# A two-block kernel: which engine does the side work of the last projection

## What is computed

```python
def swiglu_ffn(h, w_ffn_in, w_ffn_out):
    gate, up = jnp.split(h @ w_ffn_in, 2, axis=-1)
    return (jax.nn.silu(gate) * up) @ w_ffn_out

# last two lines of second_block
    y = swiglu_ffn(h, w_ffn_in[l], w_ffn_out[l])
    x = x + ga2 * rmsnorm(y, post_ffn_g[l])
```

## Time and profile before

| | |
|---|---|
| time, three runs | 1335.21 us median (1334.09 to 1336.07) |
| profiled execution | 1334.96 us, of which the span in the trace 1333.2 us |
| TensorE busy | 1313.8 us (99% of the span) |
| VectorE busy | 982.8 us (74%), 1218 instructions |
| ScalarE busy | 554.2 us (42%) |
| GpSimd busy | 88.2 us (7%) |
| granted TensorE clock | 0.999 of full (2.4 GHz) |

### The profile page before, as it was taken

One profiled execution on the slowest core, in us unless ns is written; L12 is line 12 of the kernel. 1 busy time (PEld: TensorE's weight loads), 2 busy tenths in 40 slices (PEclk: granted clock), 3 DMA queues, 4 the chain that ended last, 5 costly groups with the idle time before them and its releaser, 6 DMA issues.

```text
span 1333.2 us, 15857 instructions
## 1 busy us (share of the span) xinstructions
PE 1313.8 (99%) x6443; PEld 1065.8 (80%) x6443; DVE 982.8 (74%) x1218; ACT 554.2 (42%) x770; POOL 88.2 (7%) x153
## 2 busy tenths in 40 slices
PE   7999999999999999999999999999999999999997
PEld 4799688888888888888888777778878888888885
DVE  4787877999778777677759799866795444346988
ACT  4553444344333343222332566774443222224543
POOL 0000000000001000100000011000002210000001
PEclk9999999999999999999999999999999999999999
DMA  9544055325455546654222211122204333325565
GB/s 387 199 133 137 2 172 199 129 87 187 158 174 179 182 162 207 222 201 164 92 99 95 95 64 48 49 95 95 95 32 158 117 120 103 104 103 195 189 221 190
DMA packets 34473, 188.03 MB, mean 141 GB/s; under 512 B 4304, under 2 KB 5088, under 8 KB 18016
## 3 DMA queue, kind: packets, MB, share of 16 engines
q1 hardware_dynamic: 20976, 140.32, 29.7%
q0 software_dynamic: 13424, 46.69, 10.8%
HBM read 182.79 MB, written 4.20 MB: 140 GB/s over the span
## 4 chain that ended last, share of the span: by engine, by line
PE 84%; DVE 8%; ACT 3%; DMA 3%; issue 2%; SPq 0%; DVEq 0%; ACTq 0%
PE bank L1695 25%; PE bank L1697 24%; PE bank L1696 24%; DVE WL L947 2%; PE bank L2039 2%; PE bank L2040 2%; PE bank L2045 2%; DMA raw<-weights 1%; DMA adaf<-ada 1%; PE bank L1900 1%; DVE ada_acc L989 1%; PE bank L2235 1%; ACT WH L448 1%; PE bank L2205 1%; DVE raw L960 1%
## 5 line engine op out<-in xcount | busy, mean ns | idle before, releaser
L1695 PE MATMUL bank<-hH,WH 128*128 128x512 f32 x992 | 390.1, 393 | 0.9 <-DVE WL L947 0.5
L1697 PE MATMUL bank<-hH,WL 128*128 128x512 f32 x992 | 386.4, 390 | 0.0
L1696 PE MATMUL bank<-hL,WH 128*128 128x512 f32 x992 | 386.3, 389 | 0.0
L947 DVE TENSOR_TENSOR WL<-raw,WH 128x2048 fp32r<-128x2048 f32 (+1 forms) x114 | 253.6, 2227 | 153.8 <-ACT WH L448 153.7
L448 ACT ACTIVATE WH<-raw 128x2048 fp32r<-128x2048 f32 (+1 forms) x117 | 218.0, 1866 | 237.1 <-DMA raw<-weights 179.5
L1695 PEld LDWEIGHTS bank<-hH,WH 128*128 128x128 f32 x992 | 186.3, 188 | 42.5 <-issue 3.3
L1697 PEld LDWEIGHTS bank<-hH,WL 128*128 128x128 f32 x992 | 186.2, 188 | 39.4
L1696 PEld LDWEIGHTS bank<-hL,WH 128*128 128x128 f32 x992 | 186.4, 188 | 37.7 <-issue 0.2
L989 DVE SCALAR_TENSOR_TENSOR ada_acc<-ada_half,csil,ada_acc 128x1024 f32<-128x1024 f32 x70 | 89.7, 1281 | 4.9 <-DMA ada_half<-ada_later 2.3
L1444 DVE SCALAR_TENSOR_TENSOR cacc<-uT,vec,cacc 128x511 f32<-128x511 f32 (+29 forms) x120 | 83.3, 756 | 0.0
L401 POOL DMA_DIRECT2D ada_half<-ada_later x80 | 42.6, 532 | 569.7 <-DVE ada_acc L989 334.9
(11 more groups left out here) (360 smaller groups left out, 2176.8 us busy)
## 6 DMA issues: line engine op xcount, KB each, us to landing
raw<-weights SPq DMA_DIRECT2D x119, 1024.0 KB, 5.0
ada_half<-ada_later POOLq DMA_DIRECT2D x80, 512.0 KB, 4.5
adaf<-ada SPq DMA_DIRECT2D x8, 1024.0 KB, 19.8
xT<-x_t SPq DMA_DIRECT2D x4, 512.0 KB, 6.0
x_rows<-xB POOLq DMA_DIRECT2D x32, 64.0 KB, 2.2
gF<-x_rows POOLq DMA_DIRECT2D x3, 512.0 KB, 6.9
ctxT<-ctx_t SPq DMA_DIRECT2D x1, 1024.0 KB, 28.0
out_t<-gF SPq DMA_DIRECT2D x2, 512.0 KB, 2.6
```

Of the source, the lines that this page charges most:

```text
L947: TT_(lo_of(c, 0, width), raw_of(c, 0, width), hi_of(c, 0, width), sub).then_inc(s.lo_done, 1)
L1695: mm(o, lh, rh, start=start, stop=False, skip_group_check=skip)
L1696: mm(o, lh, rl, start=False, stop=False, skip_group_check=skip)
L1697: return mm(o, ll, rh, start=False, stop=stop, skip_group_check=skip)
```

## The change

Work moves from VectorE to GpSimd:

- the eleven `rest_lo` (768 columns each), in a loop of their own on GpSimd
- `combine(0)` and `combine(1)`, right behind them on GpSimd. `combine(2)` on VectorE now waits for them (`gain_row1` at 2)
- the upper-column products with `gpB` of tiles 0 and 1, so that GpSimd makes all four
- the last step of tile 2: instead of one fused instruction on VectorE, a `tensor_scalar` and a `tensor_tensor` of 1024 columns on GpSimd. Its store now waits for GpSimd and stands second in SyncE's queue, behind tile 3's

VectorE's tail no longer has tile 2's step in it. `BIAS_AT` and `GAIN_AT` are the new counts of the semaphore `y_scaled`, from which the two products are gone. What TensorE, ScalarE and the weight loads do is unchanged.

```diff
-BIAS_AT, GAIN_AT = (1, 2, 6, 8), (9, 10, 5, 7)
+BIAS_AT, GAIN_AT = (1, 2, 4, 6), (7, 8, 3, 5)
...
-            for n, t in enumerate((2, 3, 0)):
-                store(n + 1, t, 0, D)
+            store(s.x_new, 3 * KT + 1, 3, 0, D)
+            store(s.gain_row1, 2 + TT + 2, 2, 0, D)
+            store(s.x_new, 3 * KT + 2, 0, 0, D)
             for half in range(2):
-                store(4 + half, 1, half, CW)
+                store(s.x_new, 3 * KT + 3 + half, 1, half, CW)
...
+            pool.wait_ge(s.ffn_lo, FT + PAIRED)
+            for q in range(PAIRED):
+                pool.wait_ge(s.ffn_hi, FT + PAIRED + q + 1)
+                nc.gpsimd.tensor_tensor(gL[q][:, 4:7, :], gF[q][:, 4:7, :], gH[:, q, 0:3, :], sub)\
+                    .then_inc(s.ffn_lo, 1)
+            both, upper_rows = slice(0, 2), slice(2, 4)
+            pool.wait_ge(s.copied, GATE_COPIES + 6)
+            nc.gpsimd.tensor_tensor(parts[:, upper_rows, CW:D], parts[:, upper_rows, CW:D], parts[:, both, CW:D], add)\
+                .then_inc(s.gain_row1, 1)
+            pool.wait_ge(s.gain_row1, 1)
+            nc.gpsimd.tensor_tensor(parts[:, upper_rows, CW:D], parts[:, upper_rows, CW:D], parts[:, both, 0:CW], add)\
+                .then_inc(s.gain_row1, 1)
...
             pool.wait_ge(s.rows_in, 80)
-            for t in (2, 3):
+            for t in range(TT):
                 pool.wait_ge(s.row_ready, t + 1)
                 nc.gpsimd.tensor_tensor(piece(gained, t, 1), piece(parts, t, 1), gpB[:, CW:D], mult)\
                     .then_inc(s.gain_row1, 1)
+            pool.wait_ge(s.gain_row1, 2 + TT)
+            pool.wait_ge(s.y_scaled, 3 * KT + GAIN_AT[2])
+            pool.wait_ge(s.root_ready, 4)
+            nc.gpsimd.tensor_scalar(gained[:, 2, 0:D], gained[:, 2, 0:D], yscale[:, 2:3], None, mult)                .then_inc(s.gain_row1, 1)
+            pool.wait_ge(s.gain_row1, 2 + TT + 1)
+            nc.gpsimd.tensor_tensor(x_row(2), x_row(2), by_quarter(gained[:, 2, 0:D]), add).then_inc(s.gain_row1, 1)
...
-            def rest_lo(q):
-
-                dve.wait_ge(s.ffn_hi, FT + PAIRED + q + 1)
-                TT_(gL[q][:, 4:7, :], gF[q][:, 4:7, :], gH[:, q, 0:3, :], sub).then_inc(s.ffn_lo, 1)
...
-                if n == 0:
-                    dve.wait_ge(s.copied, GATE_COPIES + 6)
-                    own.link(TT_(parts[:, upper_rows, second_half], parts[:, upper_rows, second_half],
-                                 parts[:, both, second_half], add))
-                elif n == 1:
-                    own.link(TT_(parts[:, upper_rows, second_half], parts[:, upper_rows, second_half],
-                                 parts[:, both, first_half], add))
-                elif n == 2:
+                if n == 2:
+                    dve.wait_ge(s.gain_row1, 2)
                     dve.wait_ge(s.mm_done, 16 * C_REST)
...
-                if 2 <= i < PAIRED + 2:
-                    rest_lo(i - 2)
                 split_lo(c, split_width(c))
...
-            for t in range(2):
-                TT_(piece(gained, t, 1), piece(parts, t, 1), gpB[:, second_half], mult).then_inc(s.y_scaled, 1)
...
-            last_add(2, 0)
...
                 if x == 0:
-                    last_add(3, 1)
-            for x in range(2):
-                last_add(x, 2 + x)
+                    last_add(3, 1, 1)
+            last_add(0, 2, 1)
+            last_add(1, 3, 2)
```

More of the change, by code:

```diff
@@ L371, in _, with store @@
                 load_chunk(c)
-            def store(n, t, half, cols):
-                sp.wait_ge(s.x_new, 3 * KT + n)
+            def store(ready, n, t, half, cols):
+                sp.wait_ge(ready, n)
                 at = slice(CW * half, CW * half + cols)
@@ L1606, in _ @@
             pair_lo(PAIRED - 1)
-            def rest_lo(q):
-                dve.wait_ge(s.ffn_hi, FT + PAIRED + q + 1)
-                TT_(gL[q][:, 4:7, :], gF[q][:, 4:7, :], gH[:, q, 0:3, :], sub).then_inc(s.ffn_lo, 1)
-            both, upper_rows = slice(0, 2), slice(2, 4)
             first_half, second_half = slice(0, CW), slice(CW, D)
             def combine(n):
-                if n == 0:
-                    dve.wait_ge(s.copied, GATE_COPIES + 6)
-                    own.link(TT_(parts[:, upper_rows, second_half], parts[:, upper_rows, second_half],
-                                 parts[:, both, second_half], add))
-                elif n == 1:
-                    own.link(TT_(parts[:, upper_rows, second_half], parts[:, upper_rows, second_half],
-                                 parts[:, both, first_half], add))
-                elif n == 2:
+                if n == 2:
+                    dve.wait_ge(s.gain_row1, 2)
                     dve.wait_ge(s.mm_done, 16 * C_REST)
@@ L1647, in row_bias, with last_add @@
                 TS(ybias[:, t:t + 1], ysum[:, 2 * t + 1:2 * t + 2], 1.0 / D, EPS, mult, add).then_inc(s.y_scaled, 1)
-            def last_add(t, n):
-                if t >= 2:
-                    dve.wait_ge(s.gain_row1, t - 1)
+            def last_add(t, n, halves):
+                dve.wait_ge(s.gain_row1, 2 + t + 1)
                 dve.wait_ge(s.y_scaled, 3 * KT + GAIN_AT[t])
@@ L1655, in last_add @@
                 row = by_quarter(gained[:, t, 0:D])
-                if n < TT - 1:
-                    STT(x_row(t), row, yscale[:, t:t + 1], x_row(t), mult, add).then_inc(s.x_new, 1)
-                    return
-                for half in range(2):
-                    STT(x_half(t, half), row[:, 2 * half:2 * half + 2, :], yscale[:, t:t + 1], x_half(t, half), mult, add)\
+                by = 4 // halves
+                for half in range(halves):
+                    at = slice(by * half, by * half + by)
+                    STT(x_row(t)[:, at], row[:, at, :], yscale[:, t:t + 1], x_row(t)[:, at], mult, add)\
                         .then_inc(s.x_new, 1)
```

## The result

| | before | after |
|---|---|---|
| time, median of 15 runs each | 1334.91 us | 1337.43 us (1336.01 to 1339.06) |
| profiled execution, its span | 1334.96, 1333.2 us | 1336.49, 1334.7 us |
| TensorE, VectorE, ScalarE, GpSimd busy | 1313.8, 982.8, 554.2, 88.2 us | 1314.0, 989.9, 554.1, 135.6 us |

The change makes the kernel slower: ratio 1.0021, with a 95% interval of 1.0014 to 1.0027, so 2.5 us by the medians (0.19%). VectorE has 16 instructions less and is busy 7 us longer: the work that left it came back as standing time.

A forecast was written before the change was run, and what follows sets the result against it. TensorE, busy 99% of the span, bounds the kernel, with VectorE's chain at the end. TensorE 2.0 later less the 1.36 wait, then the tail's hold, put VectorE's end at +1.6: 1334.96 + 1.6 = 1336.6 us, range 1332.6 to 1340.0.

The forecast's parts named there:

- What leaves VectorE: Work off VectorE ends TensorE's wait of 1.36 and starts the last sum earlier: 2.1 us gained if GpSimd disturbs nobody.
- GpSimd's lengths: Times on GpSimd: 1.8 us for 768 columns, 2.35 for 1024, 1.3 for the `tensor_scalar` (at most 2.35).
- Rival C: Tail: `tensor_scalar` or its first use on GpSimd takes microseconds more; with 5 us more, 1338 us; chance 0.06.
- The hold: VectorE stands still while GpSimd reads SBUF, 2.1 ns per column: 1.56 us for 768 columns, 2.1 for 1024.
- First pass: VectorE's step becomes 4.97 us, 0.4 late at the chunk of 1272.40; TensorE starts its second pass 2.0 later.
- rival B: First pass: VectorE never catches up; eight steps take 28.1 + 8h for hold h; +4.1 us, 1339.0; chance 0.22.
- B's point: First pass: a hold above 1.51 us makes eight steps pass 40.2; each 0.1 more costs 0.8 at the copies.
- The second term: First pass, chunk of 1272.40: a low part settles between VectorE's two sums and holds it for the full 1.56 us.
- Second pass: Wide additions' holds covered, cost nothing (1 us uncovered); the wait of 1.36 goes; TensorE ends 0.6 us late.
- Tail: GpSimd's 1024-column addition from about 1323.5 holds tile 0's product or tile 3's step 2.1 us; VectorE's end +1.6.
- A: Rival for the whole change: GpSimd waits for gaps and disturbs nobody, the whole 2.1 gained, 1332.9 us; chance 0.22.

The follow-up runs named there:

- the fills: Changed kernel with each of GpSimd's eleven low parts replaced by a memset of the same 768 columns, which reads nothing: 1334.39 us, ratio 0.9999.
- the pieces: Changed kernel with each low part on GpSimd cut into three instructions of 256 columns: 1336.87 us, ratio 1.0017.

## Why the prediction was right, and where its steps failed

The forecast was 1336.6; the median is 1337.43. The direction, the mechanism (GpSimd's reads hold VectorE) and the part that pays (low parts, then tail) were right. Against its own base the forecast was +1.6, and the medians give +2.5; the profiled executions +1.5. That it came so near is in part luck, because errors of single terms cancelled: TensorE waited less at the copies than forecast and more behind them.

**What leaves VectorE, worth 2.1.** Too high. Without low parts on GpSimd the wait of 1.36 becomes 0.30, not 0, and the last sum starts 0.64 nearer to it, not the 0.7 to 0.8: 1.7 us. I gave that second part to tile 2's step; 0.40 of it comes from the two products.

**GpSimd's lengths.** 768 columns: forecast 1.8, measured 1.84 where it ran undisturbed. 1024 columns: 2.35, measured 2.39 where it began beside an idle VectorE (with the fills and with the pieces), 2.57 in the tail. `tensor_scalar` over 1024 columns: forecast 1.3, with 2.35 as an upper bound; measured 2.85 in all six runs that have it. The bound failed, not only the value. Every time VectorE ran the same two-input instructions beside its second half, so no run shows what it takes alone, and whether the 2.85 holds a wait stays open. Rival C had named this term, but with other consequences.

**The hold.** 1.56 forecast for 768 columns, 1.65 measured; 2.1 for 1024, 2.1 to 2.2 measured; 0.54 for 256 in pieces, from 0.48 in the earlier trace rows. Scaling by columns from two short rows of the attention was sound.

**First pass.** The step: 4.97 forecast, 5.06 measured. The lateness at the sums of the chunk of 1272.40: they start at 1272.82, so 0.42 + 0.53 = 0.95 late, forecast 0.4. By the formula of rival B, 28.1 + 8h with the measured 1.65 makes 41.3, that is 1.1 late. B's arithmetic was right: my h of 1.56 lay 0.05 above B's point of 1.51, and the measured one lies 0.14 above it, over eight steps. The second term failed the other way. I had the low part settle between the two sums of that chunk, for another 1.56. In the trace the two sums run at 0.68 and 1.22 and the split behind them is held (1274.67, 3.40), which delays nothing on ScalarE. That is luck of 0.03 us: the low part asked at 1273.56, the second sum had started at 1273.53, while in the two chunks before the second sum was held as forecast (2.85 and 2.75 instead of 1.22). So TensorE's wait grew by 0.94 (0.47 to 1.41), the lateness and nothing else; I had "about 2.5". The run with the low parts placed elsewhere shows the term exists (2.17), only not at that place in after.

**Second pass.** This is the step that failed. I cost the two wide additions at nothing ("without that cover it is 1 us"), and part of the cover was gone. The sums at 1289.38 and 1291.26 lost 1.15 and 2.09, their chunk's split came late, and TensorE waited 0.59 at 1296.29. And the last wait is 0.86, where I had none. I timed the last chunk by its load, which was to land at 1310.4, with VectorE free to start its sums there. In the trace that load is issued at 1304.78 and takes no more than 5.1 us, so it lands by 1309.9 (1310.4 in the time of before, as forecast), but the sums start at 1311.47, because VectorE has not been idle since 1289.38. It does catch up by 0.5 a chunk while TensorE has 18 products for each (4.08 us against 3.53), but for each of the three chunks of 12 products ahead of the last TensorE needs 2.72, less than VectorE, and `combine(2)` stands there as well. So a hold at 1289 is still there at the end. TensorE starts behind its last wait 1.37 later than before; the forecast had 0.6.

**Tail.** I had a hold of 2.1 on tile 0's product or tile 3's step. The `tensor_scalar` began at 1323.01 instead of about 1322.1 and took 2.85 instead of 1.3, which moved the addition from about 1323.5 to 1325.95, where VectorE first had a sum with a bank, which isn't held (0.69 at 1326.42), and then tile 1's product, held for the rest: 1.23. That this term is smaller than forecast, and the waits of TensorE larger, is how the sum came near.

**The rivals.** A, no disturbance, is what the first low parts did (12.37 for three, VectorE at its normal lengths), and no later one did; with the low parts' reads taken away, and the hold in the tail left, the kernel stands at 1334.39. B had the right sign and the right point, and 1.6 us too much: it took the whole length of 1.8 as the hold, and the same place term as I did. Its sign of no idle time of VectorE in the first pass came true (0.04 us of 20), its wait of over 4 us at the copies didn't. The chance for slower by over 0.2%, 0.31, stood on B; the median lies 0.5 us under its bound of 1337.9, and the ratio of 1.0021 (to 1.0027) is at 0.2% itself, so that case can't be called ruled out.

## What to carry to other kernels

Work given to GpSimd isn't taken off VectorE when both read two tensors from SBUF: a low part cost VectorE 0.87 us by itself and 1.65 us on GpSimd. Before moving a two-input instruction there, multiply its columns by 2.1 ns and compare that with the time it takes on VectorE (1.1 to 1.2 ns a column here), and don't count on gaps unless the engine is ahead of its loads when the work begins. Fills on GpSimd, instructions of VectorE that read a bank, and the one `tensor_scalar` on GpSimd held nobody here. A hold also lasts: VectorE had no idle time behind 1289, so what it lost there was still missing 25 us later. And before moving anything, try the place where the loaded engine already waits.

## What the runs showed of the hardware

**At first GpSimd was kept out, later it got its turn.** From 1229.51 to 1238.60 VectorE ran two-input instructions back to back at their normal lengths (0.68, 2.28), and GpSimd's low part that was ready at 1232.45 didn't get through: three of them took 12.37 us, where one alone takes 1.84. Only when VectorE waited 0.42 us for a load, at 1239.02, did GpSimd get in, and from then on each waiting one got its turn behind an instruction of VectorE. The pieces and the run with the low parts alone show the same (first held instruction at 1238.92 and 1240.55, each behind VectorE's first wait). So the disturbance began only where VectorE first went idle. Behind that first time no gap was needed: at 1252.58 a low part asked while VectorE ran without a pause (sums at 1251.94 and 1252.54), got in behind the sum that had just begun, and held the split at 1253.14 (3.95). Why the two stretches differ no run here shows. The Trainium skill ("SBUF — State Buffer", "Who interferes with whom") has it that the order of issue decides which side waits, for the whole instruction; the trace agrees in that nearly the whole length is lost (1.65 of 1.84, 2.1 to 2.2 of 2.39). "Order" alone doesn't foretell the first stretch, where a waiting low part was passed over by four more instructions of VectorE.

**Writes don't disturb.** Three fills of 768 columns beside two-input instructions, issued back to back, started at once, ran at 0.74 to 0.75 and held nobody. The one of 1024 in the tail ran 0.96 beside a two-input instruction and had ended before the next began. The same section of the Trainium skill says so (a GpSimd instruction that only writes doesn't contend with two-input instructions of VectorE), and the runs agree.

**Turns are by instruction, prices by column.** One instruction of 768 columns takes 1.65 us from VectorE at once, three of 256 take 0.54 each (0.43 from a sum of 1024 columns), from three different instructions.

**A one-input read held nobody.** In all six traces with the `tensor_scalar` of 1024 columns VectorE's product and its step of two SBUF inputs beside it took 0.69 and 1.28, their lengths of before. I have no explanation from these runs.

**A long wait of TensorE cost clock.** Behind a wait of 2.17 us the granted clock was 0.50 for over 3 us, in one trace; behind waits of 1.41 and less in the same place it was 1.00.
